# Three-layer fp32 network: the convolution's taps on one engine, its norm beside the output projection, norms by Ln and Exp

## What is computed

```python
u = rms_norm(h, mix_norm_g)
proj = u @ w_in                       # 1024 -> 2560
q, k, v, glu_a, glu_g = split(proj)   # 512 columns each
attn_out = moba_attention(heads(q), heads(k), heads(v), rel_bias)

def conformer_conv(a, g, w_dw, b_dw, ln_g, ln_b):
    u = a * sigmoid(g)
    u = depthwise_conv(u, w_dw, taps=31, causal) + b_dw
    mu = mean(u); var = mean(square(u - mu))          # over 512 channels
    un = (u - mu) * rsqrt(var + 1e-5) * ln_g + ln_b
    return silu(un)

mixed = concatenate([attn_out, conv_out])
h = h + mixed @ w_out
u = rms_norm(h, ffn_norm_g)
h = h + (silu(u @ w_gate) * (u @ w_up)) @ w_down
h = rms_norm(h, final_norm_g)
```

## Time and profile before

| | us |
|---|---|
| median of 3 runs | 2194.17 (2191.85 to 2194.5) |
| the profiled execution | 2194.04 |
| its span | 2192.2 |
| TensorE busy | 1942.1 (89%) |
| VectorE busy | 1092.4 (50%) |
| ScalarE busy | 837.7 (38%) |
| GpSimd busy | 194.5 (9%) |

### The profile page before, as it was taken

The page is one execution under the profiler, slowest core; times in us unless marked ns, Lnnn a source line. Parts: engine busy times, 40 slices in busy tenths (PEclk is TensorE's granted clock), DMA queues, the critical chain, the costliest instruction groups (busy, mean ns, idle before and its releaser), DMA issues.

```text
span 2192.2 us, 23655 instructions
## 1 busy us (share of the span) xinstructions
PE 1942.1 (89%) x9020; PEld 1526.5 (70%) x9020; DVE 1092.4 (50%) x1548; ACT 837.7 (38%) x1227; POOL 194.5 (9%) x170
## 2 busy tenths in 40 slices
PE   4984689999998799779899999989868899999997
PEld 2872468888885579447688888766734567888885
DVE  4499433333323444662655542266885336555423
ACT  4444523333213211552555542221185425555321
POOL 0583100000000000700000000000042000000000
PEclk8997899999999899889999999998967999999999
DMA  3411022222222222001132332321200012222321
GB/s 135 135 58 39 1 77 77 96 96 96 96 97 96 85 93 91 20 1 58 58 97 94 100 111 96 106 77 58 96 1 1 1 62 73 96 96 96 107 105 58
DMA packets 25722, 166.28 MB, mean 76 GB/s; under 512 B 3082, under 2 KB 3210, under 8 KB 6704
## 3 DMA queue, kind: packets, MB, share of 16 engines
q1 hardware_dynamic: 23904, 159.88, 21.2%
q0 software_dynamic: 1744, 5.37, 0.8%
HBM read 163.10 MB, written 2.13 MB: 75 GB/s over the span
## 4 chain that ended last, share of the span: by engine, by line
PE 80%; DVE 12%; ACT 4%; POOL 2%; issue 2%; DMA 0%; SPq 0%; POOLq 0%; ACTq 0%; DVEq 0%
PE ps L356 22%; PE ps L358 22%; PE ps L357 22%; DVE cacc L1078 3%; PE ps L389 2%; PE ps L490 2%; DVE w_lo L970 2%; PE ps L471 2%; POOL tmp L318 1%; PE ps L459 1%; DVE tmp L975 1%; ACT ring L740 1%; PE ps L371 1%; PE ps L369 1%; PE ps L370 1%
## 5 line engine op out<-in xcount | busy, mean ns | idle before, releaser
L356 PE MATMUL ps<-a_hi,w_hi 128*128 128x512 f32 x1648 | 656.4, 398 | 71.8 <-DVE a_lo L981 34.0
L357 PE MATMUL ps<-a_lo,w_hi 128*128 128x512 f32 x1648 | 649.2, 394 | 0.0
L358 PE MATMUL ps<-a_hi,w_lo 128*128 128x512 f32 x1648 | 648.9, 394 | 0.0
L356 PEld LDWEIGHTS ps<-a_hi,w_hi 128*128 128x128 f32 x1648 | 314.8, 191 | 148.2 <-issue 58.1
L357 PEld LDWEIGHTS ps<-a_lo,w_hi 128*128 128x128 f32 x1648 | 314.7, 191 | 68.2 <-issue 2.6
L358 PEld LDWEIGHTS ps<-a_hi,w_lo 128*128 128x128 f32 x1648 | 314.1, 191 | 66.8
L669 ACT CAST w_hi<-raw 128x2048 fp32r<-128x2048 f32 x82 | 155.9, 1901 | 448.2 <-PE ps L358 367.5
L970 DVE TENSOR_TENSOR w_lo<-raw,w_hi 128x2048 fp32r<-128x2048 f32 x82 | 187.7, 2290 | 266.6 <-ACT w_hi L669 266.6
L356 PE MATMUL ps<-h_hi,w_hi 128*128 128x512 f32 x528 | 207.9, 394 | 0.0
L358 PE MATMUL ps<-h_hi,w_lo 128*128 128x512 f32 x528 | 205.6, 389 | 0.0
L357 PE MATMUL ps<-h_lo,w_hi 128*128 128x512 f32 x528 | 205.4, 389 | 0.0
(11 more groups left out here) (184 smaller groups left out, 2254.8 us busy)
## 6 DMA issues: line engine op xcount, KB each, us to landing
raw<-weights_dram SPq DMA_DIRECT2D x148, 1024.0 KB, 4.9
xT<-x_in_dram SPq DMA_DIRECT2D x8, 256.0 KB, 7.2
bias_t<-bias_rows_scratch POOLq DMA_DIRECT2D x8, 256.0 KB, 4.2
ncb<-decay_rows_scratch POOLq DMA_DIRECT2D x8, 256.0 KB, 4.7
out_dram<-xT SPq DMA_DIRECT2D x8, 256.0 KB, 2.0
vec<-vectors_dram SPq DMA_DIRECT2D x1, 282.5 KB, 2.9
ring<-ramp_dram POOLq DMA_DIRECT2D x1, 260.0 KB, 4.0
tmp<-positions_dram POOLq DMA_DIRECT2D x1, 256.0 KB, 7.1
```

What stands on the lines that cost most here:

```text
L356: pe.matmul(dst, wh, hi[:, k0 + k, :], start=start and k == 0, stop=False)
L357: pe.matmul(dst, wh, lo[:, k0 + k, :], start=False, stop=False)
L358: last = pe.matmul(dst, wl, hi[:, k0 + k, :], start=False, stop=stop and k == nk - 1)
```

## The change

- **Convolution.** ScalarE's products and GpSimd's adds are gone. VectorE does all 124 taps, in an order written out as `tap_order`: nine of chunk 0, nine of chunk 1, nine of chunk 2, then whichever chunk has the fewest done. Nine are issued in each of slabs 1 to 3 of in1 (two before the weight split, seven behind it), ten in each of slabs 4 to 9 (three and seven) and three in each attention unit until they are used up.
- **Evictions.** q, k and v are moved out of PSUM by ScalarE, behind its cast of the next slab.
- **Output projection.** The sums for the convolution's norm go to banks 4 and 5. `out_half` does half of a slab's chunks: slab 0's attention half stands between the two sums, slab 1's behind the second, then both convolution halves, then slabs 2 and 3 whole.
- **No reciprocals.** All eight norms and the convolution's norm take `exp(-0.5 * ln(x))` on ScalarE in place of Sqrt on ScalarE and reciprocal on VectorE. The set `natural_log_exp_and_others` is loaded by hand at the start, before the attention of layer 1 and at the head of each output phase. Layer 3's latent norm keeps its Sqrt and reciprocal.

```diff
-    "pad", "glu_g", "glu", "taps", "prod", "ptaps", "ln_sum", "ln_act", "ln_dve", "brow_mm", "brow_ev", "masks",
+    "pad", "glu_g", "glu", "taps", "ln_sum", "ln_act", "ln_dve", "brow_mm", "brow_ev", "masks",
     "rope_dve", "rope_act",
...
-            for k in range(2 * TAPS):
-                wait("prod", k + 1)
-                if k < 2:
-                    nc.gpsimd.tensor_scalar(cacc[:, k, :], tmp[:, 2 + k, :], col("conv_b", k), None, ALU.add
-                                            ).then_inc(sem["ptaps"], 1)
-                else:
-                    wait("ptaps", k - 1)
-                    nc.gpsimd.tensor_tensor(cacc[:, k % 2, :], cacc[:, k % 2, :], tmp[:, 2 + k % 4, :], ALU.add
-                                            ).then_inc(sem["ptaps"], 1)
             wait("fg_dve", 4)
...
+            def out_half(name, j, k0, fill=lambda k: None):
+                n, o = BASE[name] + j, PAIR[name] + j
+                if k0 == 0:
+                    slab_waits(n, o)
+                for k in range(k0, k0 + 4):
+                    fill(k)
+                    for half in range(2):
+                        c = k * 256 + half * P
+                        wh, wl = w_hi[:, n % 2, c:c + P], w_lo[:, n % 2, c:c + P]
+                        dst = ps[:, 2 * (o % 2) + half, :]
+                        pe.matmul(dst, wh, a_hi[:, k, :], start=k == 0, stop=False)
+                        pe.matmul(dst, wh, a_lo[:, k, :], start=False, stop=False)
+                        last = pe.matmul(dst, wl, a_hi[:, k, :], start=False, stop=k == DC - 1)
+                if k0:
+                    last.then_inc(sem["slab"], 1)
             def out_proj(name, fill, k):
...
-            for stage in range(2):
-                for c in range(4):
-                    if stage == 0:
-                        wait("taps", 2 * TAPS)
-                        wait("ptaps", 2 * TAPS)
-                        pe.matmul(ps[:, BX, :], ones, cacc[:, c, :], start=c == 0,
-                                  stop=c == 3).then_inc(sem["ln_sum"], 1)
-                    else:
-                        wait("ln_dve", 4)
-                        wait("ln_act", c + 1)
-                        pe.matmul(ps[:, BX, :], ones, tmp[:, c, :], start=c == 0,
-                                  stop=c == 3).then_inc(sem["ln_sum"], 1)
-            out_proj("out1", "att1", 1)
+            wait("taps", 4 * TAPS)
+            for c in range(4):
+                pe.matmul(ps[:, BT, :], ones, cacc[:, c, :], start=c == 0, stop=c == 3
+                          ).then_inc(sem["ln_sum"], 1)
+            wait("oev", UNITS[1][-1].group + 1)
+            out_half("out1", 0, 0)
+            for c in range(4):
+                wait("ln_act", c + 1)
+                pe.matmul(ps[:, BT + 1, :], ones, tmp[:, c, :], start=c == 0, stop=c == 3
+                          ).then_inc(sem["ln_sum"], 1)
+            out_half("out1", 1, 0)
+            for j in range(2):
+                out_half("out1", j, 4, lambda k: wait("alo", LOWS["att1"] + k - 3))
+                if j:
+                    norm_sum(1, 0)
+                    norm_sum(1, 1)
+            for j in range(2, 4):
+                project("out1", j)
+                norm_sum(1, 2 * j - 2)
+                norm_sum(1, 2 * j - 1)
+            norm_sum(1, 6)
+            norm_sum(1, 7)
             ffn_up("up1", "norm1")
...
                 wait("sums", DC * (k + 1))
-                A.activation(tmp[:, 4, :], ps[:, BT, :], ACT.Sqrt, bias=col("eps"), scale=1.0 / D
+                A.activation(tmp[:, 4, :], ps[:, BT, :], ACT.Ln, bias=col("eps"), scale=1.0 / D
                              ).then_inc(sem["root"], 1)
+                wait("root", k + 1)
+                A.activation(tmp[:, 5, :], tmp[:, 4, :], ACT.Exp, scale=-0.5).then_inc(sem["rstd"], 1)
...
+                act.preload_act_table_set("natural_log_exp_and_others")
                 per = 3 if name.startswith("down") else 1
...
-            done_products = [0]
-            def products(count):
-                for _ in range(count):
-                    k = done_products[0]
-                    if k == 2 * TAPS:
-                        return
-                    j, c = k // 2, k % 2
-                    if j == 0:
-                        wait("glu", c + 1)
-                    if k >= 4:
-                        wait("ptaps", k - 3)
-                    A.activation(tmp[:, 2 + k % 4, :], cu[:, c, j:j + S], ACT.Copy, scale=col("conv_w", c * TAPS + j)
-                                 ).then_inc(sem["prod"], 1)
-                    done_products[0] += 1
-            def attend(run, extra=lambda: None):
+            def attend(run):
                 n, kind = len(run), run[0].kind
...
                         move(run[i])
-                        extra()
                     if kind in ("moba", "fox", "sb") and i - 2 in ends:
...
+            act.preload_act_table_set("natural_log_exp_and_others")
             for c in range(DC):
...
                 split(n + 2)
-                if j >= 2:
-                    products(6)
-            attend(runs_of(1)[0], lambda: products(1))
+                if j >= 4:
+                    wait("slab", n + 1)
+                    bank = ps[:, 2 * (o % 2):2 * (o % 2) + 2, :]
+                    if j < 8:
+                        A.activation(qk1[:, 2 * (j - 4):2 * (j - 4) + 2, :], bank, ACT.Copy,
+                                     scale=SCALE if j < 6 else 1.0).then_inc(sem["qkv"], 1)
+                    else:
+                        A.copy(v1[:, :, 256 * (j - 8):256 * (j - 7)], bank.rearrange(
+                            "p b (t c) -> p (b t) c", c=256)).then_inc(sem["qkv"], 1)
+            act.preload_act_table_set("natural_log_exp_and_others")
+            attend(runs_of(1)[0])
             for c in range(4):
...
             wait("ln_sum", 8)
-            A.activation(tmp[:, 4, :], ps[:, BX, :], ACT.Sqrt, bias=col("ln_eps"), scale=1.0 / 512
+            A.activation(tmp[:, 4, :], ps[:, BT + 1, :], ACT.Ln, bias=col("ln_eps"), scale=1.0 / 512
                          ).then_inc(sem["ln_act"], 1)
+            wait("ln_act", 5)
+            A.activation(tmp[:, 5, :], tmp[:, 4, :], ACT.Exp, scale=-0.5).then_inc(sem["ln_act"], 1)
             for c in range(4):
-                wait("ln_dve", 6 + c)
+                wait("ln_dve", 5 + c)
                 A.activation(tmp[:, c, :], cacc[:, c, :], ACT.Silu, bias=col("ln_b", c),
                              scale=col("ln_g", c)).then_inc(sem["ln_act"], 1)
-                wait("ln_act", 6 + c)
+                wait("ln_act", 7 + c)
                 A.copy(a_hi[:, 4 + c, :], tmp[:, c, :]).then_inc(sem["ahi"], 1)
...
-            def reciprocal_root(k):
-                wait("root", k + 1)
-                Vv.reciprocal(tmp[:, 5, :], tmp[:, 4, :]).then_inc(sem["rstd"], 1)
-                wait("rstd", k + 1)
             def low(c, src, n):
...
             def normed(k, name, a):
-                reciprocal_root(k)
+                wait("rstd", k + 1)
                 for c in range(DC + 1):
...
             def normed_residual(k):
-                reciprocal_root(k)
+                wait("rstd", k + 1)
                 for c in range(DC):
...
+            tap_order, latest = [], {}
+            for lo, hi, n in ((0, 1, 9), (0, 2, 9), (0, 3, 9), (0, 4, 4 * TAPS - 27)):
+                for _ in range(n):
+                    done = [sum(c == d for d, _ in tap_order) for c in range(4)]
+                    c = min(range(lo, hi), key=lambda c: (done[c], c))
+                    tap_order.append((c, done[c]))
             done_taps = [0]
...
                     k = done_taps[0]
-                    if k == 2 * TAPS:
+                    if k == 4 * TAPS:
                         return
-                    j, c = k // 2, 2 + k % 2
+                    c, j = tap_order[k]
                     src = cu[:, c, j:j + S]
...
                     else:
-                        wait("taps", k - 1)
+                        wait("taps", latest[c])
                         Vv.scalar_tensor_tensor(out=cacc[:, c, :], in0=src, scalar=col("conv_w", c * TAPS + j),
...
                     done_taps[0] += 1
+                    latest[c] = k + 1
...
                                      ).then_inc(sem["glu"], 1)
-                elif j < 8:
-                    move_features("in1", j, qk1[:, 2 * (j - 4):2 * (j - 4) + 2, :],
-                                  SCALE if j < 6 else 1.0)
+                    taps(0 if j == 0 else 2)
                 else:
-                    move_tokens("in1", j, v1, 256 * (j - 8))
+                    taps(3)
                 split(BASE["in1"] + j + 2)
...
                     Vv.tensor_copy(brow[:, 512:640], ps[0:HEADS, 7, 0:P]).then_inc(sem["brow_ev"], 1)
-                if j >= 4:
-                    taps(10)
-            taps(2)
+                else:
+                    taps(7)
             wait("bias_out", 16 * HEADS)
-            attend(runs_of(1)[0])
```

(10 more changed lines are left out.)

## The result

| | before | after |
|---|---|---|
| median | 2194.34 us (4 runs, 2191.85 to 2195.93) | 2130.63 us (4 runs, 2127.78 to 2131.21) |
| profiled span | 2192.2 us | 2129.0 us |
| mean granted clock of TensorE | 0.938 | 0.946 |

The ratio is 0.971, 95% interval 0.969 to 0.973: faster by 63.7 us in the medians and 63.2 us in the profiled spans. The forecast was 2131.0 us, a span of 2129.1.

What follows compares the result with a forecast made beforehand. The prediction saw a TensorE-led chain (80%) interrupted by waits, with VectorE's taps slowed by GpSimd. 41.1 us through out1 plus 22.0 from the other norms made 63.1 off the 2192.2 span: 2129.1, forecast 2131.0 us, range 2121 to 2143.

Steps and rivals of the forecast that it cites:

- norm0: First norm: with the table loaded early, Ln and Exp replace Sqrt, table load and reciprocal; 4.0 us less.
- first score: End of in1: VectorE takes up the first attention score at 159.3 instead of 196.28, 37.0 us ahead.
- attention: Layer 1's attention: VectorE, with 37 added taps, becomes the bound; 59.7 us instead of 46.2, 13.5 given back.
- conv norm and out1: From the last attention value through out1: reordered sums and half slabs keep TensorE fed; 17.6 us less.
- norms 1, 4, 5, 6: At these norms Ln and Exp finish before VectorE's split, so the reciprocal falls out; 3.3 us less each.
- norms 2 and 3, together: Norm 2 loses its whole reciprocal, 3.3 us; norm 3, with no split before it, gives 2.7.
- norm7: Last norm: the reciprocal goes, an Exp comes, the table load lies beside the last sums; 2.8 us less.
- the price of a tap: In in1 and the attention: each VectorE tap costs 0.67 us, the low end of 0.67 to 1.71.
- the 1.9 for stalls: In the attention: 1.9 us added for small stalls, from 0 up to the first-listed rival.
- The first rival: Attention hurt more than counted: TensorE's clock near 0.63, 9 us lost, out1 starting at half clock; 2141 us, chance 0.17.
- The third: Rival on the norms: two tables serve Ln and Exp, two loads per norm, 16 us given back; 2147, chance 0.03.
- the cover of 5.4 us: In out1: half a slab of matmuls, 5.4 us, hides the 4.9 us chain behind the squares' sums.

Runs made afterwards that it cites:

- beside_scalar: The changed kernel plus 62 unused products on ScalarE, placed as in the kernel before; 2130.21 us.
- beside_gpsimd: The changed kernel plus 62 unused two-source adds on GpSimd, free-running from the first gated chunk on; 2204.29 us.
- beside_late: The changed kernel plus 20 unused two-source adds on GpSimd that start after tap 60; 2144.04 us.
- undo_taps: The changed kernel with convolution and evictions as before (ScalarE products, GpSimd adds, 62 VectorE taps, evictions on VectorE); 2152.05 us.
- serial_out1: The changed kernel with both sums of the convolution's norm first and then the whole output projection; 2142.79 us.
- evict_vector: The changed kernel with the six evictions of q, k and v back on VectorE, taps as changed; 2130.64 us.
- more_taps: The changed kernel with 97 taps in in1 instead of 87, none behind the last split, two per attention unit instead of three; 2115.65 us.
- no_preload: The changed kernel without the hand-placed table loads that it added; 2141.17 us.
- no_att_taps: The changed kernel without the 37 taps of the attention, leaving the convolution incomplete; 2116.20 us.
- undo_norms: The changed kernel with Sqrt and reciprocal in all eight norms and the convolution's, without the added table loads; 2158.75 us.

## Why the prediction was right

| step | forecast | measured |
|---|---|---|
| norm0 | 4.0 ahead | 2.5 |
| first score | 159.3 (37.0 ahead) | 160.78 (35.5) |
| attention | 59.7, values end 219.0 (23.5) | 57.8, 218.55 (23.9) |
| conv norm and out1 | 54.7 (41.1) | 54.2 (42.0) |
| norms 1, 4, 5, 6 | 3.3 each | 3.4, 3.3, 3.4, 3.4 |
| norms 2 and 3, together | 6.0 | 6.1 |
| norm7 | 2.8 | 2.7 |
| sum | 63.1 | 63.2 |

Leads in brackets are differences between the start times of the same instruction in the two traces; at out1 that is the start of its last sums, and norm1's is taken at the first matmul behind it. The table load for the Sqrt of layer 3's latent norm, taken at 0 between 0 and 1.3, cost nothing (the lead was 57.14 us at the slab before it and 57.05 behind it).

**Norm0** was mis-sized. Of the 1.5 missing, 0.7 is not the change's: the sums ended at 22.82 instead of 22.15, and in the twelve runs above, whose code up to there is nearly the same, anywhere from 21.69 to 23.18. The other 0.8 is a cover that I did not look behind. Before, ScalarE's cast of slab 0 (1.9 us) ran beside the reciprocal; now VectorE is ready at once, and the chain goes through that cast: `ACT w_hi` from 24.17 to 25.95, then `ACT a_hi`. I had named what hides the edit in each other norm, and not asked here what the reciprocal itself had hidden.

**In1**: the taps cost 0.67, and TensorE did not wait for VectorE, as the 108.00 of 108 us show. The first score is late by what norm0 lacked. The choice that carried the forecast was the price of a tap, and beside_scalar, beside_gpsimd, beside_late and undo_taps show its reason: the adds on GpSimd. But "GpSimd's adds" is the coarse form of it: one-source additions on GpSimd cost a tap 0.18 us and two-source ones 1.04.

**Attention**: the bound was named rightly (VectorE busy 51.75 of 57 us; taps taken out shorten it) and the size was 1.9 too long. From the first score to the last scaling 51.3 us passed, against 52.1 of work counted: the 1.9 for stalls did not come. The last stretch took 6.4 instead of 5.7, and that is a matter of the clock. In the changed kernel and in serial_out1, whose attention is the same code (columns as above):

```profile
212.00:218.50 6.50, 6.48 (x59) 4.88 (x56) 1.65 (x4) 3.17 (x7) 0.00 (x0) 0.74 0.02 4
```

```profile
212.00:217.00 5.00, 4.98 (x57) 3.74 (x56) 1.56 (x3) 3.08 (x8) 0.00 (x0) 1.00 0.02 5
```

At a clock of 1.00 the same work takes 4.95 us (211.99 to 216.94), at 0.74 it takes 6.44. This difference of 1.5 us goes through to the end of the kernel, and a like one (1.35 at the values' end) is most of the 2.2 us that evict_vector's span seemed to gain.

**The first rival** (the attention hurt more, clock near 0.63) was wrong: the clock there was 0.82, and VectorE kept its pace through it. It priced "a matmul at half clock" at 0.79 us, which is the duration of the first one behind a wait; at half clock they follow each other every 0.43 us. In more_taps, with less waiting, the clock in the attention was 0.90. **The third** (two loads in each norm) is what no_preload makes true: the change holds because the set is loaded by name before.

**Conv norm and out1**: the cover of 5.4 us was enough for the chain of 4.9 (no TensorE gap, 24.00 of 24). serial_out1 gives the price of the order by itself, 13.9 of the 18.1 us by which this stretch is shorter.

**Norms**: each was worth what the rows said, but one thing was left out. At norm1 the wait of TensorE shrank from 10.4 to 7.0 us, and it still restarts at half clock and in this execution stays there longer (13 matmuls of 0.43 us in its chain instead of 8). The shorter wait alone does not make it so: behind the same 7.0 us it is 8 in more_taps and 10 in evict_vector and serial_out1. The lead grew by 3.4 at the first matmul and only by 2.5 at slab 1 of up1 (44.42 - 41.97). So 0.9 us was lost there that I had not counted, 1.5 at norm0, and the attention and out1 gave 2.4 more than counted: that the sum came within 0.1 us is partly luck.

## What to carry to other kernels

Before an operation is moved between engines, price it from a stretch in which the engines beside it do what they will do afterwards: the same tap cost 0.67, 0.85 and 1.71 us in these kernels, by what GpSimd did. Count how full the engine is at each stage, not overall: moving taps out of the stage where VectorE is the bound, and from behind the last split ahead of it, into slabs with 0.7 to 2.6 us to spare, gave another 15 us, and an offload that is worth nothing today (the evictions) is worth 4 to 5 us once that room is used. And where a long operation is removed, ask what ran in its shadow: here a cast of 1.9 us, which took back 0.8 of the gain.

## What the runs showed of the hardware beyond that

- A one-source tensor_scalar on VectorE beside back-to-back two-source adds on GpSimd took 77.14 us once, until the last of 62 adds, and about 1.5 us twice in the kernel before; alone it takes 0.54, beside one-source additions 0.78. What decides between the two was not settled.
- A two-source scalar_tensor_tensor beside the same adds went from 0.67 to 1.71 us, a two-source subtraction of 2048 columns from 2.29 to 2.82 and 3.38, and the adds from 1.22 to 1.81.
- An instruction that reads PSUM did not suffer: in the kernel before, an eviction of 1024 columns took 1.21 us beside GpSimd's adds (at 119.47) and 1.22 without.
- The same last stretch of the attention, with TensorE busy all through it, ran at a granted clock of 1.00 in serial_out1, evict_vector, more_taps and no_att_taps, and at 0.74, 0.73 and 0.64 (a mix of the levels 2.4 and 1.2 GHz) in the changed kernel, beside_scalar and undo_norms. What decides it was not settled.
